# Spreading the second group's output products in a one-core hybrid decoder layer

## The reference

```
h = x + concat[A, B, C, D](rmsnorm(x) @ w_in) @ w_out     # B is the RWKV-7 state recurrence
q  = rmsnorm(h) @ wq ; s1 = q[:, :, 0] @ k1 ; s2 = q[:, :, 1] @ k2
e, g = top-16 of (top-16 of s1) + (top-16 of s2), softmax of the scores
hsel = dot(u_tab[e], rmsnorm(h)) ; out = sum(g * gelu(hsel) * v_tab[e])
y = rmsnorm(h + out)
```

## Time and profile before

| what | value |
|---|---|
| time, median of 3 runs | 1734.12 us (1733.38 to 1738.78) |
| the profiled execution's own time | 1734.5 us |
| its span, first to last instruction | 1732.7 us |
| PE, DVE, ACT, POOL busy | 71%, 72%, 40%, 53% |
| data moved | 602.42 MB, 348 GB/s over the span |
| mean granted clock of TensorE | 0.843 of full |

### The profile page before, as it was taken

One profiled execution on the slowest core, in us unless ns is written; L12 is line 12 of the kernel. 1 busy time (PEld: TensorE's weight loads), 2 busy tenths in 40 slices (PEclk: granted clock), 3 DMA queues, 4 the chain that ended last, 5 costly groups with the idle time before them and its releaser, 6 DMA issues.

```text
span 1732.7 us, 19380 instructions
## 1 busy us (share of the span) xinstructions
PE 1232.9 (71%) x5360; PEld 619.5 (36%) x5360; DVE 1241.3 (72%) x2955; ACT 698.0 (40%) x1986; POOL 910.8 (53%) x1134
## 2 busy tenths in 40 slices
PE   5997898567777767767976767675766667666555
PEld 4886766322333333322322323232322222222110
DVE  3568755688887877768586778676767777767774
ACT  3321113455444444334345445343433343434444
POOL 0155120467576566555366656555656655656762
PEclk9999899778899898878986778778888887768878
DMA  6321147999999999999799999999999999999996
GB/s 173 122 98 49 37 137 100 318 390 418 414 415 416 407 418 419 417 417 398 255 388 417 419 417 416 417 378 418 419 417 418 418 418 412 409 417 402 420 415 255
DMA packets 110636, 602.42 MB, mean 348 GB/s; under 512 B 24752, under 2 KB 27184, under 8 KB 43968
## 3 DMA queue, kind: packets, MB, share of 16 engines
q0 software_dynamic: 74880, 545.29, 76.8%
q1 hardware_dynamic: 35648, 55.90, 11.0%
HBM read 597.96 MB, written 3.19 MB: 347 GB/s over the span
## 4 chain that ended last, share of the span: by engine, by line
DMA 39%; PE 27%; DVE 15%; POOL 6%; ACT 5%; issue 5%; DVEq 3%; POOLq 0%; SPq 0%; ACTq 0%
DMA arena<-in_uv,arena 38%; PE ps L985 10%; DVE arena L1848 8%; PE ps L553 5%; POOL arena L2072 4%; DVE arena L1320 3%; DVEq L1317 3%; PE ps L600 2%; POOL arena L2071 2%; PE ps L906 2%; PE ps L591 2%; DVE arena L1326 2%; PE ps L613 1%; PE ps L925 1%; ACT arena L1284 1%
## 5 line engine op out<-in xcount | busy, mean ns | idle before, releaser
L985 PE MATMUL ps<-arena 128*64 128x512 f32 x2048 | 662.8, 782 | 407.9 <-ACT arena L1284 407.7
L1848 DVE CUSTOM_DVE_ANT_0 arena<-arena 128x1024 f32<-128x1024 f32 x520 | 641.0, 1234 | 303.8 <-DMA arena<-in_uv,arena 285.0
L2072 POOL DMA_INDIRECT arena<-in_uv,arena x520 | 622.7, 1198 | 90.5 <-POOL arena L2071 8.7
L2071 POOL TENSOR_TENSOR arena<-arena 1x1 f32<-1x1 f32 x520 | 207.1, 398 | 534.9 <-PE ps L985 404.8
L985 PEld LDWEIGHTS ps<-arena 128*64 128x64 f32 x2048 | 152.1, 166 | 798.2 <-ACT arena L1284 553.2
L1278 ACT ACTIVATE arena<-arena 128x1 f32<-128x1 f32 x520 | 105.3, 202 | 757.3 <-DVE arena L1848 755.8
L1284 ACT ACTIVATE arena<-arena 128x64 f32<-128x64 f32 (+1 forms) x520 | 181.5, 349 | 17.0
L1280 ACT ACTIVATE arena<-arena 128x1 f32<-128x1 f32 x520 | 153.2, 295 | 16.9
L1320 DVE TENSOR_TENSOR arena<-arena 128x512 f32<-128x512 f32 (+7 forms) x310 | 132.6, 429 | 28.1 <-ACT arena L1032 18.9
L553 PE MATMUL ps<-arena 128*128 128x264 f32 (+1 forms) x608 | 141.9, 389 | 0.7 <-DVE arena L1320 0.7
L906 PEld LDWEIGHTS ps<-arena 128*128 128x128 f32 x1024 | 121.9, 198 | 34.9 <-issue 33.4
(11 more groups left out here) (161 smaller groups left out, 973.8 us busy)
## 6 DMA issues: line engine op xcount, KB each, us to landing
arena<-in_win SPq DMA_DIRECT2D x38, 512.0 KB, 3.3
arena<-in_wqk SPq DMA_DIRECT2D x64, 256.0 KB, 7.5
arena<-in_uv,arena POOLq DMA_INDIRECT x520, 12.3
arena<-in_wout SPq DMA_DIRECT2D x16, 512.0 KB, 7.8
arena<-in_xp SPq DMA_DIRECT2D x4, 512.0 KB, 7.5
arena<-in_wqk SPq DMA_DIRECT2D x16, 128.0 KB, 9.5
out_yp<-arena SPq DMA_DIRECT2D x4, 512.0 KB
arena<-in_const SPq DMA_DIRECT2D x1, 928.0 KB, 4.5
```

The source lines that it names most:

```text
L985: last = mm(ps[64 * q:64 * q + 64, b + c, :], diag[:, (s + q) % 8, :], ring[:, (s + q) % RING, D + 512 * c:D + 512 * c + 512], start=(s == ...
L1848: v.tensor_tensor_reduce(out=ring[:, s % RING, 0:D], in0=ring[:, s % RING, 0:D], in1=row, scale=1.0, scalar=0.0, op0=MUL, op1=ADD, accum_o ...
L2071: pool.tensor_tensor(carrier[:, 1:2], carrier[:, 0:1], carrier[:, 0:1], ALU.add).then_inc(S["carried"], 1)
L2072: pool.indirect_dma_start(out=ring[:, s % RING, :], out_offset=None, in_=a["uv"][:, :], in_offset=bass.IndirectOffsetOnAxis(ap=idx[:, t, s ...
```

## The change

`pace` becomes `3 * k // 4`. The output products and all steps behind them get new numbers for group 1: the six half products stand at steps +0, +4, +7, +11, +14 and +18 from `C_OUT` (before: +0, +1, +3, +4, +6 and +7), the transposes at +19 to +29, the last pair copy of ACT at +40 (before +28). Group 0 keeps its numbers. SP waits for `slot_used` 144 + 2j before it issues block j.

```diff
+W_SLOT = 144
 def pace(k):
-    return 2 * k // 3
+    return 3 * k // 4
...
                     sp_.wait_ge(S["y_mm"], 2 * GC)
                     for j in range(KT):
+                        sp_.wait_ge(S["slot_used"], W_SLOT + 2 * j)
                         sp_.dma_start(w_blocks[j], a["wout"][:, OUT_ORDER[j], :]).then_inc(d_wb, 16)
...
-                for k in range(2):
-                    yield C_OUT + 3 * k
+                step = 7 if g else 3
+                for k in range(len(tiles)):
+                    yield C_OUT + step * k
                     project(k, 0)
-                    yield C_OUT + 3 * k + 1
+                    yield C_OUT + step * k + (4 if g else 1)
                     project(k, 1)
-                if g:
-                    yield C_OUT + 6
-                    project(2, 0)
-                yield C_OUT + 7
-                if g:
-                    project(2, 1)
+                for k in range(len(tiles)):
+                    for half in range(2):
+                        yield C_OUT + (19 if g else 7) + 4 * k + 2 * half
+                        turned(k, half)
...
                 for k, t in enumerate(tiles):
-                    yield C_OUT + 3 * k + 3
+                    yield C_OUT + (7 * k + 7 if g else 3 * k + 3)
                     act.wait_ge(S["x1_done"], t + 1)
                     squares(t, "sq2", xn2[t])
-                    yield C_OUT + 3 * k + 5
+                    yield C_OUT + (7 * k + 9 if g else 3 * k + 5)
                     root(t, "mean2", t + 1, "root2")
...
+                yield C_OUT + 6
+                residual(2)
...
+                yield C_OUT + 13
+                residual(3)
...
+                yield C_OUT + 20
+                residual(TILES)
+                second_features(2, 0)
...
+                yield C_OUT + 30
+                second_features(TILES, 1)
```

More of the change, by code:

```diff
@@ L791, in turned @@
                     turn_half(t, half, 7)
-                for k in range(2):
-                    yield C_OUT + 3 * k
+                step = 7 if g else 3
+                for k in range(len(tiles)):
+                    yield C_OUT + step * k
                     project(k, 0)
-                    yield C_OUT + 3 * k + 1
+                    yield C_OUT + step * k + (4 if g else 1)
                     project(k, 1)
+                for k in range(len(tiles)):
+                    for half in range(2):
+                        yield C_OUT + (19 if g else 7) + 4 * k + 2 * half
+                        turned(k, half)
                 if g:
-                    yield C_OUT + 6
-                    project(2, 0)
-                yield C_OUT + 7
-                if g:
-                    project(2, 1)
-                turned(0, 0)
-                yield C_OUT + 9
-                turned(0, 1)
-                yield C_OUT + 11
-                turned(1, 0)
-                yield C_OUT + 13
-                turned(1, 1)
-                if g:
-                    yield C_OUT + 15
-                    turned(2, 0)
-                    yield C_OUT + 17
-                    turned(2, 1)
-                    yield C_OUT + 19
+                    yield C_OUT + 31
                     pe.wait_ge(S["hT2_done"], 2 * TILES + 2)
@@ L1159, in mixer @@
                 for k, t in enumerate(tiles):
-                    yield C_OUT + 3 * k + 3
+                    yield C_OUT + (7 * k + 7 if g else 3 * k + 3)
                     act.wait_ge(S["x1_done"], t + 1)
                     squares(t, "sq2", xn2[t])
-                    yield C_OUT + 3 * k + 5
+                    yield C_OUT + (7 * k + 9 if g else 3 * k + 5)
                     root(t, "mean2", t + 1, "root2")
                 if g:
-                    yield C_OUT + 20
+                    yield C_OUT + 32
                     act.wait_ge(S["xrep_mm"], 1)
@@ L1169, in mixer @@
                     for k in range(8):
-                        yield C_OUT + 21 + k
+                        yield C_OUT + 33 + k
                         if k % 4 == 0:
@@ L1572, in mixer @@
                 lk(tt(y_, y_, gg[g], MUL).then_inc(S["rwkv_out"], 1))
-                t0 = 2 * g
-                yield C_OUT + 2
-                residual(t0)
-                yield C_OUT + 4
-                second_mean(t0)
-                yield C_OUT + 5
-                residual(t0 + 1)
+                if g == 0:
+                    yield C_OUT + 2
+                    residual(0)
+                    yield C_OUT + 4
+                    second_mean(0)
+                    yield C_OUT + 5
+                    residual(1)
+                    yield C_OUT + 6
+                    second_norm(0)
+                    yield C_OUT + 7
+                    second_mean(1)
+                    yield C_OUT + 8
+                    second_features(0, 0)
+                    yield C_OUT + 9
+                    second_norm(1)
+                    yield C_OUT + 10
+                    second_features(0, 1)
+                    yield C_OUT + 12
+                    second_features(1, 0)
+                    yield C_OUT + 14
+                    second_features(1, 1)
+                    return
@@ L1595, in mixer @@
-                yield C_OUT + 12
-                if g:
-                    second_norm(TILES)
-                second_features(t0 + 1, 0)
-                yield C_OUT + 14
-                second_features(t0 + 1, 1)
-                if g:
-                    yield C_OUT + 16
-                    second_features(TILES, 0)
-                    yield C_OUT + 18
-                    second_features(TILES, 1)
+                second_mean(2)
+                yield C_OUT + 10
+                second_norm(2)
@@ new lines, in mixer @@
+                yield C_OUT + 13
+                residual(3)
+                yield C_OUT + 15
+                second_mean(3)
+                yield C_OUT + 17
+                second_norm(3)
+                yield C_OUT + 20
+                residual(TILES)
+                second_features(2, 0)
+                yield C_OUT + 22
+                second_mean(TILES)
+                second_features(2, 1)
+                yield C_OUT + 24
+                second_norm(TILES)
+                second_features(3, 0)
@@ L1607, in _ @@
+                yield C_OUT + 26
+                second_features(3, 1)
+                yield C_OUT + 28
+                second_features(TILES, 0)
+                yield C_OUT + 30
+                second_features(TILES, 1)
             cw = col("cw", 0, 2 * CK).rearrange("p (a b) -> p a b", b=CK)
```

11 lines of the change are left out of this document (removed).

## The result

The changed kernel takes 1740.12 us (median of 8 runs, 1737.33 to 1745.09); the kernel before takes 1735.76 us beside it (8 runs, 1733.38 to 1738.78). The ratio is 1.0028, with an interval of 1.0014 to 1.0041: 2.4 to 7.1 us slower. 1728.2 was forecast, and faster was given the largest chance. The profiled run took 1740.74 us, with a span of 1739.0.

The account below looks back on a forecast made before the run. The kernel waits for data: transfers bound it, and the product stretch loses 22.3 us. 1734.5 - 9.3 (products and weights) + 3.0 (chain), with later steps at zero, gave 1728.2 us, range 1718 to 1745.

Parts of the forecast that it names:

- Part 1: Output products, halves set apart: 9.3 us of dry time outside the first gap, to be scaled by 1.16.
- the first gap: Dry transfers after the first half product: 4.1 us if it starts at 39.2, 1.9 at 37 (taken), none at 35.
- The gap behind the fifth half: Dry transfers after query, fifth half product and pair: 4.8 us, the worst spot.
- the prediction's best end: Dry 10.8 and chain 0 give 1723 us; with query weights filling the gap at the fifth half, 1717.
- the rival of cold products: Half products after pauses run at 1.2 GHz, 13.5 us each instead of 7.13: 1757 us, chance 0.05.
- Part 2: Output weights issued later: landed at t = 37 to 39.2, PE waits 6 to 8.5 us at the first half product.
- t: Time in us from the end of the pair of slots 150 and 151, which is t = 0.
- the prediction's own tally: List of PE and ring times around the products; it read a factor 1.16 too low for the kernel before.
- the rival "weights late": Blocks land at t = 42 or later, the first gap is 7 us or more: no change, 1734 us, chance 0.30.
- Part 3: Chain at three steps for four slots: more waits between engines cost 3.0 us, ends 0 and 23.
- The rival "the chain starves the ring": In the chain DVE catches up late, PE frees pairs later, buffers run dry: 11 us, 1743 us, chance 0.20.
- Part 4: Steps behind the products, moved later: no one waits, zero; 5 us where the cover failed one slot each.

Follow-up runs that it names:

- Experiment 10: The kernel of experiment 6 with its half products at +0, +2, +5, +7, +10 and +12: 1736.01 us, ratio 0.9991 to the kernel before.
- experiment 1: Changed kernel with all eight weight blocks in one burst, one key load sooner, without slot waits: 1731.56 us, ratio 0.9968 to the kernel before.
- experiment 2: Changed kernel with PE_AHEAD 2 in place of 3, nothing else: 1728.3 us, ratio 0.9947 to the kernel before.
- experiment 8: Changed kernel with ACT's copy of u one step earlier, PE_AHEAD left at 3: 1731.92 us, ratio 0.9964 to the kernel before.
- experiment 6: Changed kernel with the changes of experiment 1 and experiment 2 together: 1722.53 us, ratio 0.9916 to the kernel before.
- experiment 11: The kernel before with PE_AHEAD 2 and nothing else: 1740.71 us, ratio 1.0016 to the kernel before.
- experiment 3: Changed kernel with the old pace, 2 * k // 3, the rest of the change kept: 1729.5 us, ratio 0.9943 to the kernel before.

## Why the prediction was wrong

**Part 1, products apart: right, and better than forecast.** Outside the first gap 9.3 x 1.16 = 10.8 us of dry time were forecast; the windows 780 to 860 lose 16.4 us in all, 9.4 of them the first gap, which leaves 7.0. The gap behind the fifth half, put at 4.8 us and as the worst spot, is within the 2.1 us of 840 to 860: query weights (0.52 MB from 841 to 845) fill part of it, as the prediction's best end had allowed. The halves took 7.04 to 7.13 us and the first 8.70 (9.0 forecast), so the rival of cold products didn't come up. Experiment 10 is the counter-test: narrower, and 12.9 us of loss are back.

**Part 2, weights late: the step that failed.** The prediction said: "So PE waits 6 to 8.5 us", and "It only makes the first gap: 4.1 us if the start is 39.2, 1.9 at 37, none at 35". PE waited 15.96 us and the first gap was 9.4, in a window that lost 11.0. The first gap is the term that was mis-sized. Three of its times were off, all to the same side:
- PE reached the half at t = 25.1, not 30.7. I had let the four pairs come 7.5 us apart, as in the earlier trace rows while the weights travelled. But their eight gathers were all issued by 738.83, next to the first block (737.75), and the three steps from the first pair to the last took 15.2 us (742.89 to 758.11), not 22.6. The first pair came later than forecast, 6.2 us after t = 0 and not 4.4: ACT's root of the head norm at 739.91 stood in front of the diagonal of slot 153.
- The weights had landed at t = 41.1, not 37 to 39.2: 40.0 us from the first issue at 737.75, where the earlier trace rows gave 36.2.
- The last gather in flight ended at t = 44.9, not 49.2 (a number that the prediction gives without its working). It is bound to the pair before the half: as PE came 5.6 us sooner and stopped, so the ring ended sooner.

The half and the pair behind it (8.70 + 1.94 us), the restart and this earlier end make up the gap: transfers again from t = 54.3, which is 9.4 us after 44.9. The restart took 2.6 us behind the pair (788.3 to 790.9) where the earlier trace rows gave 3.1. The late landing alone would have made the gap some 6 us by the prediction's own tally (4.1 at 39.2, and 1.9 more to 41.1); the rest comes from PE standing earlier. So the rival "weights late" (t = 42 or later, dry 18.9 us, no change) described the place; with t = 41.1 the total, 16.4 us, lay between forecast (13.0) and rival, by a smaller part 1 and a larger gap. Experiments 1 and 2 took the wait away and got 10 and 14 us back, the second with the 5.0 us of the chain in it.

**Part 3, the chain: right in kind, mis-sized.** 3.0 us were forecast, 5.1 measured (slots 0 to 144). I had counted waits (33 before, 42 after) as alike and put the extra loss into the early steps. What costs is four of them, two slots long, in the inverse's levels, where PE stands 4 to 8 us each; the trace of the kernel before could not show them, since the old pace had them one slot long. Experiments 2 and 8 remove them in two ways (382.8 and 381.9), and experiment 6 keeps DVE as full at 418 GB/s, against DVE as their cause. Length alone does not price a wait either: by the step numbers the kernel before had six waits of two slots elsewhere, and removing them (experiment 11) gave nothing. The rival "the chain starves the ring" had this mechanism at 11 us; it was half of that.

**Part 4, later steps: zero, right in the changed kernel** (775.4 us against 775.7 behind slot 224). Its cover, "PE runs late", held at this pace even with the weights in time (experiment 1: no wait at the third half). At the old pace it fails, and the third half waits 4.22 us (experiment 3). One of its dates was off by the step numbers: the last copy of the kernel before falls on slot 224, not 222. Nothing hangs on it.

**The sum.** By slots, + 5.1 + 10.8 - 14.3 - 0.3 is 1.3 us, or 1.1 by the last column, where -6.3 was forecast. The forecast gain of parts 1 and 2 together was 9.3 us; the slots show 3.5 (14.3 - 10.8), the windows 5.9 (22.3 - 16.4). The medians say + 4.4 for the whole, and 2.4 to 7.1 by the interval. Some 3 us between slots and medians are thus open. It is not in the tail: behind slot 519 both profiles have 13 us. A single profile and the median of its kernel differ by as much elsewhere (the table gives experiment 8 a gain of 5.7 us, its ratio 11; experiment 6 15.6 against 19.4), so its cause stays open.

1740.12 lies inside the stated range of 1718 to 1745, but the forecast gain isn't there: the first gap took 9.4 us where 2.2 were forecast (1.9 x 1.16), which alone turns the forecast gain of 6.3 us into a loss of 0.9; the chain's 2.1 us more add to it, and the 3.8 us fewer of part 1 take from it. By this count the sum is -0.8 us, where the slots show + 1.3 and the medians + 4.4. So the gain is gone by each of them; that the kernel is slower rests on the medians, and by the slots on 1 us.

## What to carry to other kernels

When a schedule is compressed, all deadlines come sooner, those of transfers too: list for each load the time from issue to need, and for each wait between engines how many slots it spans, before and after the change. Ask not when a late load lands but how long the consumer stands, since an empty ring must be refilled behind it; and date the consumer by the work that is already in flight in front of it, not by the pace that holds while the load travels. A number that shifts one engine against the others, like `PE_AHEAD` here, is to be set again with the pace: it gave nothing before the change (1.0016) and 0.81% after it.

## What the runs showed of the hardware

- Issuing the blocks apart changed nothing: with the last block issued 4.1 or 18.2 us behind the first, PE waited 16.19 and 15.96 us. Eight blocks of 512 KB took 40.0 us from first issue to last landing beside the gathers in the changed kernel and 36.2 in the kernel before. Most of the difference lies in front of the first landing (13.0 and 8.1 us after its issue); from there the other seven took some 27 and 28 us, 3.8 to 4.0 us a block.
- A half product behind a pause of PE took 8.70 us (after 15.96 us) and 9.94 (after 14.27), and 8.51 after only 4.22 us (experiment 3), against 7.13 at a granted clock of 1.00; the next one was at 7.13 again. In the changed kernel the granted clock was 0.50, the level of 1.2 GHz, while PE stood (761.9 to 777.7) and in the first 2 us of the half, and 0.91 on average over the rest of it.
- Once the ring was empty, transfers were back at full rate 2.6 us (changed kernel) and 3.1 us (kernel before) behind the pair that freed the buffers.
- With the same instructions up to there, slot 0 started anywhere from 319.7 to 326.1 us in twelve profiles. Times from a mark inside the program (here 520 dot products) leave that scatter out: 1400.0 and 1400.1 for the two profiles of the kernel before. Their stretches still differ by up to 1.4 us, and by 2.5 us in the chain of experiments 6 and 10.
